# Gate products of two tiles as seven half-size block products, with the block sums on VectorE

## Chip, cores and metric

One core of one Trainium2 chip. The metric is the device time of one execution in microseconds (us); lower is better. All data are 32-bit floats.

## What is computed

A two-layer latent block with a small context stream, followed by a third attention block. The change touches one place of the two layers, the gated merge of three branches:

```
def merge_branches(o_a, o_b, o_c, gate_logits, w_branch, w_out):
    g_a, g_b, g_c = jnp.split(jax.nn.sigmoid(gate_logits), 3, axis=-1)
    merged = g_a * (o_a @ w_branch[0]) + g_b * (o_b @ w_branch[1]) + g_c * (o_c @ w_branch[2])
    return merged @ w_out
...
p = h @ w_in[l]                 # the last 3 * 1024 columns of p are the gate logits
...
mod = silu_c @ w_ada[l] + b_ada[l]      # 6 * 1024 modulation values for each layer
```

`h` has 1024 features. The first layer (`l = 0`) works on 512 latent and 256 context tokens together, 768; the second (`l = 1`) on 512 at this place.

## The kernel before

Every engine gets its own instruction list, unrolled from one list of jobs, `PLAN[l]`, that `plan_layer` writes for each layer (the job's first word is its kind). Each engine runs its part of the jobs strictly in that order, and semaphores tie the engines together: `full`/`free` for the PSUM places, and an `event` counter for each kind of result. On VectorE and ScalarE, `V.do`/`A.do` also wait for each instruction's own end before the next.

The dense part of a layer comes after attention: four `conv_b` jobs, and then for the branches 2, 0 and 1 and the eight 128-feature tiles of each a `gate` job and a `branch` job. On TensorE (PE) a `gate` is 8 matmuls deep (1024 input features) over all tokens; a matmul handles at most 512 tokens, so in layer 0 it is 8 of 512 and 8 of 256 columns. A `branch` is 4 deep. ScalarE (ACT) takes the sigmoid of a gate tile into one of two places of `probT`, and VectorE (DVE) multiplies it with the branch product and adds it into `merged`. Then `gate_used` says that the place of `probT` is free.

In layer 0, `with_modulation` spreads 40 `acc` jobs over the dense part. Each is four VectorE instructions on a 128x1024 piece of `w_ada` that multiply it by the conditioning vector and add it up (`accumulate`). After four of them, a `rsum` (PE sums over partitions, ACT copies) and an `adag` (PE turns, DVE writes `mod`) finish the group.

Weights arrive through `ring`, six places of 1 MB. SyncE (SP) issues the loads in the order of first use; the load into a place waits until the piece that was there has been used (`chunk_prev`, `chunk_end`). `gate` pieces hold two tiles, and so do `branch` pieces.

Of the kernel before, what the change touches and what calls it, by code (L numbers as in the profile page):

```python
# [105 lines left out]
def program(nc, x, c, ctx_in, c_ctx, w_ada, b_ada, g_mix, g_ffn, w_in, qg_a, kg_a, qg_b, kg_b, sink_b, conv_w,  # L106
            w_branch, w_out, w_router, w_e_gate, w_e_up, w_e_down, norm_gain_2, w_in_2, q_norm_a_2, k_norm_a_2,
            sinks_a_2, q_norm_b_2, k_norm_b_2, w_out_2, consts, out):
    with ExitStack() as stack:
# [96 lines left out]
        back = [obuf[:, n * D:(n + 1) * D] for n in (3, 4, 5)] + [merged[:, n * D:(n + 1) * D] for n in (1, 2, 3)]  # L206
        iota = con[:, C_IOTA:C_IOTA + NX]
# [225 lines left out]
        def plan_layer(l):  # L433
# [5 lines left out]
            gates = {br: [(w, l, br, d) for d in range(KD) for w in ("gate", "branch")] for br in range(3)}  # L439
            dense = conv + gates[2] + gates[0] + gates[1]  # L440
# [12 lines left out]

        PLAN = {0: plan_layer(0), 1: plan_layer(1), 2: plan_second()}
# [10 lines left out]
        def event(name, keys):  # L465
            return Count(sem(name), keys)
# [39 lines left out]
        sig_ready = event("gate_sigmoid", of("gate", "silg"))  # L506
# [169 lines left out]
        chunk_key = {}  # L676

# [89 lines left out]
        def chunk_of(j):  # L767
# [13 lines left out]
            if kind == "gate":  # L781
                return ("gate", l, t, j[3] // 2), j[3] % 2
# [39 lines left out]
        WEIGHTED = ("qk", "v", "conv_c", "conv_x", "conv_b", "gate", "branch", "silg", "side", "wout", "wt")  # L822
# [113 lines left out]
        def _(pe):  # L936
# [81 lines left out]

            def run(j):
# [40 lines left out]
                elif kind in ("conv_c", "conv_x") or kind == "silg" and j in job:  # L1060
                    pass
                elif kind in ("qk", "conv_b", "gate", "silg", "branch", "wout"):
# [693 lines left out]
        def _(act):  # L1756
# [59 lines left out]
            def run(j):  # L1816
# [849 lines left out]
```

## Time and profile before

| | |
|---|---|
| time, median of 3 runs | 3112.27 us (3110.53 to 3115.92) |
| the profiled execution | 3114.2 us, its span 3112.4 us |
| PE busy | 2984.3 us, 96% |
| DVE busy | 1052.1 us, 34% |
| ACT busy | 613.1 us, 20% |
| layer 0, dense part | 438.14 to 872.34 us of the span |
| layer 1, gates and branches | 1950.3 to 2194.2 us, less the first gates |

Busy shares are means over stages with different limits. What a change is worth in one stage is read from that stage's instructions in order of time: which engine had something to wait for, and for whom.
### The profile page before, as it was taken

What the parts mean: (1) busy time and instruction counts of PE and PEld (TensorE: products, weight loads), DVE (VectorE), ACT (ScalarE), POOL (GpSimd) and SP (SyncE); (2) the same over time, 40 slices, a digit from 0 to 9 for tenths busy, and PEclk for the clock granted to TensorE, in tenths of its full rate; (3) what the DMA queues carried; (4) which work ended last, traced back from release to release, by engine and by line L of the source; (5) the groups of instructions that cost most, each with busy time, mean ns of one, the idle gap of its engine ahead of it and who ended that gap; (6) DMA issues with size and microseconds to landing.
All of it is one profiled execution on the core that took longest, in us unless ns stands there. A gap on an engine that the chain in (4) does not pass through costs nothing.

```text
span 3112.4 us, 32607 instructions
## 1 busy us (share of the span) xinstructions
PE 2984.3 (96%) x13043; PEld 1404.1 (45%) x13043; DVE 1052.1 (34%) x1566; ACT 613.1 (20%) x1121; POOL 75.0 (2%) x88
## 2 busy tenths in 40 slices
PE   7999999999999999999999999999979898899999
PEld 4565655555545222222335655444433222234547
DVE  4764645556514000000147554011121010137352
ACT  3135530000003010111031453000011101021161
POOL 1000000000000010101000000000000000000000
PEclk9999999999999999999999999999999999999999
DMA  8120013434413999999870201222489999963200
GB/s 251 41 82 14 15 55 128 176 135 157 161 41 140 397 351 380 355 371 380 298 200 1 68 21 46 68 81 95 162 333 408 408 408 407 408 221 81 68 1 28
DMA packets 266076, 578.83 MB, mean 186 GB/s; under 512 B 62040, under 2 KB 140136, under 8 KB 265800
## 3 DMA queue, kind: packets, MB, share of 16 engines
q1 hardware_dynamic: 258064, 554.09, 48.8%
q0 software_dynamic: 7552, 22.61, 2.4%
q8 instruction: 106, 1.74, 0.2%
q14 instruction: 42, 0.34, 0.0%
q10 hardware_dynamic: 312, 0.05, 0.0%
HBM read 561.49 MB, written 15.20 MB: 185 GB/s over the span
## 4 chain that ended last, share of the span: by engine, by line
PE 84%; DMA 11%; DVE 3%; issue 1%; ACT 1%; SPq 0%; DVEq 0%; POOL 0%; ACTq 0%; POOLq 0%
PE ps L1016 31%; PE ps L1420 9%; PE ps L1535 6%; PE ps L1032 5%; PE ps L1432 5%; PE ps L1080 5%; PE ps L1248 3%; PE ps L1260 3%; PE ps L1294 3%; DMA ring<-in_w_e_up 3%; PE ps L1093 2%; DMA ring<-in_w_e_down 2%; DMA ring<-in_w_e_gate 2%; PE ps L1056 2%; PE ps L1476 2%; PE ps L1230 1%
## 5 line engine op out<-in xcount | busy, mean ns | idle before, releaser
L1016 PE MATMUL ps<-hT,ring 128*128 128x512 f32 (+1 forms) x2080 | 773.2, 529 | 3.0 <-ACT hT L1761 2.9
L1016 PEld LDWEIGHTS ps<-hT,ring 128*128 128x128 f32 x2080 | 394.9, 191 | 367.6 <-issue 343.7
L1420 PE MATMUL ps<-ring,hT 128*64 128x512 f32 x1392 | 333.1, 607 | 17.2 <-DMA ring<-in_w_e_up 11.9
L1420 PEld LDWEIGHTS ps<-ring,hT 128*64 128x64 f32 x1392 | 89.7, 137 | 220.1 <-issue 219.3
L1032 PE MATMUL ps<-hT,ring 128*128 128x512 f32 (+1 forms) x448 | 181.5, 533 | 0.7 <-DVEq L1746 0.7
L1761 ACT ACTIVATE prob<-ps 128x512 f32<-128x512 f32 (+1 forms) x67 | 46.4, 693 | 681.0 <-PE ps L1016 681.0
L1432 PE MATMUL ps<-ring,hT 128*32 128x512 f32 x1392 | 167.4, 598 | 0.5 <-ACT hT L1761 0.5
L1535 PE MATMUL ps<-ring,hT 128*64 128x512 f32 x640 | 150.4, 603 | 15.0 <-DMA ring<-in_w_e_down 10.8
L1761 ACT ACTIVATE prob<-prob,nms 128x768 f32<-128x768 f32 (+5 forms) x224 | 159.2, 711 | 18.9 <-DVE nms L2384 8.6
L1080 PE MATMUL ps<-merged,ring 128*128 128x512 f32 (+1 forms) x384 | 142.7, 526 | 3.1 <-issue 3.1
L1016 PE MATMUL ps<-obuf,ring 128*128 128x512 f32 (+1 forms) x384 | 143.4, 523 | 0.0
L1260 PE MATMUL ps<-con,prob 128*128 128x128 f32 x872 | 140.2, 283 | 1.3 <-DVE merged L2408 0.5
L1260 PEld LDWEIGHTS ps<-con,prob 128*128 128x128 f32 x872 | 96.4, 140 | 89.5 <-issue 78.8
L2534 DVE TENSOR_TENSOR qbuf<-qbuf,ps 128x1536 f32<-128x1536 f32 x8 | 14.0, 1754 | 341.1 <-ACT qbuf L1761 341.1
L1761 ACT ACTIVATE hT<-ps,mod,amp 128x256 f32<-128x256 f32 (+1 forms) x96 | 50.7, 528 | 327.7 <-PE ps L1470 182.1
L2596 DVE SCALAR_TENSOR_TENSOR xT<-ps,mod,xT 128x512 f32<-128x512 f32 x40 | 30.0, 751 | 249.2 <-PE ps L1476 248.8
L1925 ACT COPY merged<-ps 128x512 f32<-128x512 f32 (+1 forms) x128 | 71.5, 559 | 169.9 <-PE ps L1260 129.9
L2296 DVE TENSOR_TENSOR prob<-prob,ps 128x768 f32<-128x768 f32 (+1 forms) x32 | 26.2, 820 | 231.6 <-PE ps L1016 231.6
L1248 PE MATMUL ps<-kbuf,obuf 64*128 64x256 f32 (+2 forms) x576 | 100.9, 464 | 2.5 <-DVEq L1746 2.2
L1080 PEld LDWEIGHTS ps<-merged,ring 128*128 128x128 f32 x384 | 71.2, 190 | 70.5 <-issue 67.4
L1016 PEld LDWEIGHTS ps<-obuf,ring 128*128 128x128 f32 x384 | 72.4, 190 | 66.2 <-issue 63.3
L1294 PE MATMUL ps<-merged,vbuf 128*64 128x256 f32 x736 | 96.7, 390 | 0.9 <-DVE merged L2408 0.9
(333 smaller groups left out, 3029.0 us busy)
## 6 DMA issues: line engine op xcount, KB each, us to landing
ring<-in_w_e_gate SPq DMA_DIRECT2D x95, 1024.0 KB, 12.3
ring<-in_w_e_up SPq DMA_DIRECT2D x83, 1024.0 KB, 9.7
ring<-in_w_e_down SPq DMA_DIRECT2D x76, 1024.0 KB, 9.4
ring<-in_w_in SPq DMA_DIRECT2D x49, 1024.0 KB, 5.3
ring<-in_w_ada SPq DMA_DIRECT2D x48, 1024.0 KB, 7.3
ring<-in_w_e_down SPq DMA_DIRECT2D x32, 512.0 KB, 7.2
ring<-in_w_in SPq DMA_DIRECT2D x48, 256.0 KB, 4.7
merged<-in_w_e_up SPq DMA_DIRECT2D x12, 1024.0 KB, 15.1
```

What stands on the lines that cost most here:

```text
L1016: mm = pe.matmul(ps[:, b + a:b + e], lhs[:, k, :], rhs[:, k, a:e], start=k == 0, stop=k == nk - 1)
L1032: mm = pe.matmul(ps[:, BANK[SIDE]:BANK[SIDE] + hi - lo], ring3(slot)[:, k, m % 2 * P:(m % 2 + 1) * P], h3[:, k, lo:hi], start=k == 0, stop ...
L1056: mm = pe.matmul(ps[:, b:b + CH], o2[:, k, t * P:(t + 1) * P], ring3(slot)[:, k, :], start=k == 0, stop=k == KD - 1)
L1080: mm = pe.matmul(ps[:, b:b + e - a], w[:, k, :], m3[:, k, a:e], start=k == 0, stop=k == KD - 1)
L1248: mm = pe.matmul(ps[:, b[a] + c0:b[a] + c0 + w], q[r, u["g"], u["q0"]:u["q0"] + P], k[r, u["kj"], k0:k0 + w], start=True, stop=True)
L1260: mm = pe.transpose(ps[:, o:o + P], scored(j[1], j[2], a, u)[:, m * P:(m + 1) * P], ident)
L1294: mm = pe.matmul(out_, v(tiles[m], col), exp_, start=m == 0, stop=m == len(tiles) - 1, tile_position=(0, a * HD))
L1420: mm = pe.matmul(ps[e * CX:(e + 1) * CX, b + h * 512:b + (h + 1) * 512], lhs, second_weights(slot_of[sub], e, h), start=k == 0, stop=k == ...
L1432: mm = pe.matmul(ps[q:q + CC, b + 1024:b + 1536], lhs, second_weights(slot_of[k % 2], e, h), start=k == 0, stop=k == KD - 1, tile_position ...
L1535: mm = pe.matmul(to, lhs[:, k, s0:s0 + CX], second_weights(slot, e, h), start=k == 0, stop=k == KD - 1, tile_position=(0, e * CX))
L1761: return sc.activation(o, i, f, **kw)
L1925: A.do(sc.copy(*turned_to(j)), tb_done[r], j)
```

## The change

Two gate tiles of one ring piece become one job `gate2`. The 1024 input features are cut into two halves, the two tiles are two halves of the output features, and the tokens are cut into two halves. A product of 2x2 by 2x2 blocks needs eight block products; the change computes seven, of sums of blocks:

```
P1 = A11 B11    P2 = A12 B21    P3 = S4 B22    P4 = A22 T4
P5 = S1 T1      P6 = S2 T2      P7 = (A11 - A21)(B22 - B12)
```

Here A are the weight blocks, B the token blocks, S sums of weight blocks and T sums of token blocks. A block product is 4 matmuls of 384 columns in layer 0 and of 256 in layer 1. PE runs them in the order 1, 6, 5, 7, 2, 4, 3 and accumulates some of them on top of others in PSUM, after VectorE has read what was there. The parts:

- `hsum`, once a layer on VectorE: the sums of token blocks (3 instructions on all of 4 feature groups, 4 on one each). PE waits for it before the first P1.
- `wsum`, once a pair on VectorE: 4 instructions of 512 columns, the sums of weight blocks. It stands between the two `branch` jobs of the pair before. PE waits for it before P6.
- `gate2` on VectorE: 5 instructions of half the tokens (`u2`, `u3`, `22`, `21`, `12`), on ACT one copy and four sigmoids. P7 waits for `u2`, P2 for the copy, P4 for `u3`, P3 for `22`; `u2` waits for P6, `u3` for P7, `21` for P4, `12` for P3.
- In layer 0 the last two ring places hold sums of token blocks, so the dense part's loads go round four places.
- `with_modulation` counts a `gate2` as two jobs and puts no `acc` behind a `wsum` or behind the second `branch` of a pair.

```diff
@@ with_modulation
+            def long(j):
+                return {"hsum": 0, "wsum": 0, "gate2": 2}.get(j[0], 1)
...
-            count, passed, share = len(todo), 0, len(jobs) - 4
+            count, passed, share = len(todo), 0, sum(map(long, jobs)) - 4
...
-                passed += 1
+                passed += long(j)
                 while due and due[0][0] <= passed:
                     order.append(due.pop(0)[1])
+                if j[0] == "wsum" or j[0] == "branch" and j[3] % 2:
+                    continue
                 while todo and (count - len(todo)) * share < passed * count:
@@ plan_layer
-            gates = {br: [(w, l, br, d) for d in range(KD) for w in ("gate", "branch")] for br in range(3)}
-            dense = conv + gates[2] + gates[0] + gates[1]
+            pairs = [(l, br, n) for br in (2, 0, 1) for n in range(KD // 2)]
+            dense = conv + [("hsum", l), ("wsum",) + pairs[0]]
+            for at, (_, br, n) in enumerate(pairs):
+                dense += [("gate2", l, br, n), ("branch", l, br, 2 * n)]
+                dense += [("wsum",) + p for p in pairs[at + 1:at + 2]] + [("branch", l, br, 2 * n + 1)]
@@ loads, layer 0: places of the ring from hsum to the first wout
+                        if few[0]:
+                            add_chunk(key, chunk_dmas(key), few[1] % (RING - 2))
+                            few[1] += 1
@@ TensorE
+                times("p1", a, w[:, 0:4, 0:P], h3[:, 0:4, 0:half], True)
+                need(weight_sums_ready, ("wsum",) + j[1:])
+                times("p6", b, s2, t2, True)
+                times("p5", c, s1, t1, True)
+                need(seven_added, j[1:] + ("u2",))
+                times("p7", b, w[:, 0:4, P:2 * P], h3[:, 0:4, half:2 * half], False)
+                need(first_product, j[1:])
+                times("p2", a, w[:, 4:8, 0:P], h3[:, 4:8, 0:half], False)
+                need(seven_added, j[1:] + ("u3",))
+                times("p4", b, w[:, 4:8, P:2 * P], t4, False)
+                need(seven_added, j[1:] + ("22",))
+                times("p3", c, s4, h3[:, 4:8, half:2 * half], False)
@@ VectorE
+                elif kind == "hsum":
+                    V.do(v.tensor_tensor(t1, b12, b11, ALU.subtract))
+                    V.do(v.tensor_tensor(t2, b22, t1, ALU.subtract))
+                    for k in range(4):
+                        V.do(v.tensor_tensor(t4[k], b21[:, k, :], t2[:, k, :], ALU.subtract))
+                    V.do(v.tensor_tensor(b12, b22, b12, ALU.subtract), token_sums_ready, j)
+                elif kind == "wsum":
+                    dve.wait_ge(w_full[slot], value)
+                    V.do(v.tensor_tensor(s1, a21, a22, ALU.add))
+                    V.do(v.tensor_tensor(s2, s1, a11, ALU.subtract))
+                    V.do(v.tensor_tensor(s4, a12, s2, ALU.subtract))
+                    V.do(v.tensor_tensor(a21, a11, a21, ALU.subtract), weight_sums_ready, j)
+                elif kind == "gate2":
+                    V.need(first_product, j[1:])
+                    V.need(seven_full, j[1:] + ("p6",))
+                    V.do(v.tensor_tensor(c12, p1, second, ALU.add), seven_added, j[1:] + ("u2",))
+                    V.need(seven_full, j[1:] + ("p7",))
+                    V.do(v.tensor_tensor(c22, p1, second, ALU.add), seven_added, j[1:] + ("u3",))
+                    V.do(v.tensor_tensor(c22, c22, third, ALU.add), seven_added, j[1:] + ("22",))
+                    V.need(seven_full, j[1:] + ("p4",))
+                    V.do(v.tensor_tensor(p1, p1, second, ALU.add), seven_added, j[1:] + ("21",))
...
+                    V.need(seven_full, j[1:] + ("p3",))
+                    V.do(v.tensor_tensor(c12, c12, third, ALU.add), seven_added, j[1:] + ("12",))
```

The order of VectorE in layer 0, in the middle of branch 2. Before, between two tiles (`merged<-prob,ps` is the end of a `branch`; four instructions on `ring,silc` are one `acc`; `mod` is `adag`):

```order
L2293 TENSOR_TENSOR merged<-prob,ps 128x768
L2171 TENSOR_TENSOR mod<-ps,pv 128x8 x2
L2159 SCALAR_TENSOR_TENSOR vbuf<-ring,silc,vbuf 128x1024 x4
L2293 TENSOR_TENSOR merged<-prob,ps 128x768
L2159 SCALAR_TENSOR_TENSOR vbuf<-ring,silc,vbuf 128x1024 x4
L2157 TENSOR_SCALAR kbuf<-ring,silc 128x1024
L2157 TENSOR_SCALAR prob<-ring,silc 128x1024
L2159 SCALAR_TENSOR_TENSOR kbuf<-ring,silc,kbuf 128x1024
L2159 SCALAR_TENSOR_TENSOR prob<-ring,silc,prob 128x1024
L2293 TENSOR_TENSOR merged<-prob,ps 128x768
```

After the change, from the third pair's `12` (the first row, which waits for P3) to the `wsum` of the fourth pair (the last four rows):

```order
L2414 TENSOR_TENSOR prob<-prob,ps 128x384
L2259 TENSOR_TENSOR mod<-ps,pv 128x8 x2
L2247 SCALAR_TENSOR_TENSOR vbuf<-ring,silc,vbuf 128x1024 x8
L2422 TENSOR_TENSOR merged<-prob,ps 128x768
L2245 TENSOR_SCALAR kbuf<-ring,silc 128x1024
L2245 TENSOR_SCALAR prob<-ring,silc 128x1024
L2247 SCALAR_TENSOR_TENSOR kbuf<-ring,silc,kbuf 128x1024
L2247 SCALAR_TENSOR_TENSOR prob<-ring,silc,prob 128x1024
L2394 TENSOR_TENSOR kbuf<-ring 128x512
L2395 TENSOR_TENSOR vbuf<-kbuf,ring 128x512
L2396 TENSOR_TENSOR prob<-ring,vbuf 128x512
L2397 TENSOR_TENSOR ring<-ring 128x4x128
```

All `acc` instructions of a pair now stand between the last sum of one pair and the weight sums of the next; over the whole of layer 0 there are 36 `acc` jobs in eleven such stretches (2, 4, 3, 3, 4, 3, 3, 4, 3, 3 and 4), and the other four stand ahead of `hsum`.

The order of TensorE at a similar place. Before, two tiles, each a gate of 8 and 8 matmuls and a branch of 4 and 4 (`qbuf` holds the convolution's output; the L1150 row is an `adag`):

```order
L1016 MATMUL ps<-hT,ring 128x512 x8
L1016 MATMUL ps<-hT,ring 128x256 x8
L1150 MATMUL ps<-con,sq_rs 128x4 x4
L1016 MATMUL ps<-qbuf,ring 128x512 x4
L1016 MATMUL ps<-qbuf,ring 128x256 x4
L1016 MATMUL ps<-hT,ring 128x512 x8
L1016 MATMUL ps<-hT,ring 128x256 x8
L1016 MATMUL ps<-qbuf,ring 128x512 x4
L1016 MATMUL ps<-qbuf,ring 128x256 x4
```

After, one pair: P1; P6; P5; P7 and P2 (the row of 8); P4 in two rows; P3; the `adag`; and two branches:

```order
L1080 MATMUL ps<-hT,ring 128x384 x4
L1080 MATMUL ps<-ring,vbuf 128x384 x4
L1080 MATMUL ps<-ring,kbuf 128x384 x4
L1080 MATMUL ps<-hT,ring 128x384 x8
L1080 MATMUL ps<-ring 128x384 x2
L1080 MATMUL ps<-sq_rs,ring 128x384 x2
L1080 MATMUL ps<-hT,prob 128x384 x4
L1231 MATMUL ps<-con,sq_rs 128x4 x4
L1058 MATMUL ps<-qbuf,ring 128x512 x4
L1058 MATMUL ps<-qbuf,ring 128x256 x4
L1058 MATMUL ps<-qbuf,ring 128x512 x4
L1058 MATMUL ps<-qbuf,ring 128x256 x4
```

The gates of both tiles now stand ahead of both branches, so between P3 of one pair and P6 of the next, PE has two branches and P1 to run.

The order of SP's loads behind the first pair, before (each row one piece of weights; `w_in` are gates, `w_ada` accumulations; in brackets, whose progress the load waits for):

```order
L1598 DMA ring<-in_w_ada 128x2x1024 [waits psum_full0]
L1598 DMA ring<-in_w_ada 128x2x1024 [waits modulation_chunk_used]
L1598 DMA ring<-in_w_in 128x8x256 [waits modulation_chunk_used]
L1598 DMA ring<-in_w_ada 128x2x1024 [waits psum_full1]
L1598 DMA ring<-in_w_branch 128x4x256 [waits modulation_chunk_used]
```

And after:

```order
L1682 DMA ring<-in_w_in 128x8x256 [waits seven_products_full]
L1682 DMA ring<-in_w_ada 128x2x1024 [waits modulation_chunk_used]
L1682 DMA ring<-in_w_ada 128x2x1024 [waits psum_full2]
L1682 DMA ring<-in_w_ada 128x2x1024 [waits modulation_chunk_used]
L1682 DMA ring<-in_w_branch 128x4x256 [waits seven_products_full]
```

With four places, the fourth load behind a gate piece waits for that pair's P3, which here is the next pair's gate piece and then that pair's own branch piece.

## Rows read from the trace of the kernel before

**Rows 1.** The page: busy times of the engines, and PE in 40 slices (tenths)

```profile
PE 2984.3 (96%) x13043; PEld 1404.1 (45%) x13043; DVE 1052.1 (34%) x1566; ACT 613.1 (20%) x1121; POOL 75.0 (2%) x88
...
PE   7999999999999999999999999999979898899999
```

**Rows 2.** Busy times in the two dense parts (window, length, engines, clock, DMA, GB/s)

```profile
438.14:872.34 434.20, 434.18 (x1523) 255.37 (x1521) 240.16 (x229) 26.59 (x35) 0.00 (x0) 1.00 0.42 144
1950.30:2194.20 243.90, 243.90 (x569) 107.75 (x567) 26.17 (x38) 15.61 (x25) 0.00 (x0) 1.00 0.25 76
```

**Rows 3.** Timeline of PE, layer 0 (start, length, instruction; idle before it in brackets)

```profile
675.92 10.59 PE L1016 MATMUL ps<-hT,ring 128*128 128x512 f32 x32
686.35 5.32 PE L1016 MATMUL ps<-obuf,ring 128*128 128x512 f32 x16
691.60 0.64 PE L1140 MATMUL ps<-kbuf,ones 128*32 128x256 f32 x8
...
703.02 0.95 PE L1150 MATMUL ps<-con,sq_rs 128*128 128x4 f32 x8
```

**Rows 4.** Timeline of PE: layer 1, and sixteen matmuls of 256 columns in layer 0

```profile
2008.72 7.03 PE L1016 MATMUL ps<-hT,ring 128*128 128x512 f32 x16
2015.58 3.60 PE L1016 MATMUL ps<-qbuf,ring 128*128 128x512 f32 x8
...
952.76 7.07 PE L1080 MATMUL ps<-merged,ring 128*128 128x256 f32 x32
959.77 0.61 PE L1177 MATMUL ps<-xT,prob 128*16 128x256 f32 x2
```

**Rows 5.** Timeline of DVE in layer 0

```profile
661.76 0.37 DVE L2171 TENSOR_TENSOR mod<-ps,pv 128x8 f32<-128x8 f32 x2
...
670.20 1.28 DVE L2159 SCALAR_TENSOR_TENSOR kbuf<-ring,silc,kbuf 128x1024 f32<-128x1024 f32 x1
671.52 1.29 DVE L2159 SCALAR_TENSOR_TENSOR prob<-ring,silc,prob 128x1024 f32<-128x1024 f32 x1
676.04 0.95 DVE L2296 TENSOR_TENSOR prob<-prob,ps 128x768 f32<-128x768 f32 x1 [3.23 <-PE ps L1016]
...
678.13 1.28 DVE L2159 SCALAR_TENSOR_TENSOR kbuf<-ring,silc,kbuf 128x1024 f32<-128x1024 f32 x1
...
683.41 1.54 DVE L2157 TENSOR_SCALAR vbuf<-ring,silc 128x1024 f32<-128x1024 f32 x2
```

**Rows 6.** DVE groups by form, 438 to 2200 us (busy, mean ns, idle before)

```profile
L2534 DVE TENSOR_TENSOR qbuf<-qbuf,ps 128x1536 f32<-128x1536 f32 x8 | 14.0, 1754 | 341.1 <-ACT qbuf L1761 341.1
...
L2330 DVE TENSOR_TENSOR hT<-hT 128x512 f32<-128x512 f32 x7 | 4.8, 692 | 0.9
...
L2204 DVE TENSOR_TENSOR hT<-xT,sq_rs 128x256 f32<-128x256 f32 x8 | 3.4, 426 | 0.3
```

**Rows 7.** Timeline of PE around its longest idle time

```profile
2280.39 1.04 PE L956 MATMUL ps<-of_expert,prob 128*128 128x16 f32 x4 [12.13 <-DVE prob L2457]
2282.34 5.41 PE L950 MATMUL ps<-con 128*128 128x512 f32 x8 [0.91 <-DVEq L1750]
...
40.76 19.50 PE L1016 MATMUL ps<-hT,ring 128*128 128x512 f32 x46 [2.22 <-ACT hT L1761]
```

**Rows 8.** Windows at the same places; the granted clock stands behind POOL

```profile
42.00:46.00 4.00, 4.00 (x5) 1.43 (x5) 3.83 (x5) 3.83 (x6) 0.00 (x0) 0.50 1.01 269
46.00:50.00 4.00, 4.00 (x10) 1.86 (x9) 3.66 (x9) 3.80 (x7) 0.00 (x0) 0.92 0.98 221
...
2270.00:2275.00 5.00, 0.00 (x0) 0.00 (x0) 4.76 (x10) 0.00 (x0) 0.00 (x0) 0.72 1.01 387
...
2280.00:2285.00 5.00, 3.70 (x7) 2.10 (x8) 0.81 (x5) 0.00 (x0) 1.67 (x2) 0.50 0.65 213
2285.00:2290.00 5.00, 3.00 (x8) 1.16 (x7) 0.00 (x0) 0.00 (x0) 0.31 (x1) 0.92 0.56 196
```

**Rows 9.** DMA issues in layer 0's gates (KB each, median us to landing)

```profile
ring<-in_w_ada SPq DMA_DIRECT2D x23, 1024.0 KB, 7.3
```

More of the change, by code:

```diff
@@ L676, in program @@
         chunk_key = {}
+        few, after_sums = [False, 0], []
         def second_place(r):
@@ L780, in chunk_of @@
                 return (kind, l, t // 2), t % 2
-            if kind == "gate":
-                return ("gate", l, t, j[3] // 2), j[3] % 2
+            if kind in ("gate2", "wsum"):
+                return ("gate", l, t, j[3]), 0
             if kind == "branch":
@@ L820, in chunk_dmas @@
             return plain(w_out[l], n * CH)
-        WEIGHTED = ("qk", "v", "conv_c", "conv_x", "conv_b", "gate", "branch", "silg", "side", "wout", "wt")
+        WEIGHTED = ("qk", "v", "conv_c", "conv_x", "conv_b", "gate2", "wsum", "branch", "silg", "side", "wout", "wt")
         def chunk_keys(j):
@@ L1017, in product, with seven_products, times @@
                 part(mm, key)
+            def seven_products(j):
+                l = j[1]
+                half = (NT, NX)[l] // 2
+                cn, slot = weights(chunk_of(j)[0])
+                if j[1:] == PAIRS_FIRST[l]:
+                    need(oT_ready, ("O", l, 2 * TILES[l] - 1))
+                    need(token_sums_ready, ("hsum", l))
+                a = begin(j)
+                b = a + 512
+                third = (HEAD_SUMS, SIDE)[j[3] % 2]
+                c = begin(j + ("c",), third)
+                w = ring3(slot)
+                s1, s2, s4 = weight_sums
+                t1, t2, t4 = token_sums[l]
+                def times(name, bank, lhs, rhs, first):
+                    for k in range(4):
+                        mm = pe.matmul(ps[:, bank:bank + half], lhs[:, k, :], rhs[k] if name == "p4" else rhs[:, k, :],
+                                       start=first and k == 0, stop=k == 3, skip_group_check=not first)
+                    mm.then_inc(seven_full.sem, 1)
+                times("p1", a, w[:, 0:4, 0:P], h3[:, 0:4, 0:half], True)
[10 more added lines that the diff above has]
+                times("p3", c, s4, h3[:, 4:8, half:2 * half], False)
+                chunk_end[cn] = (seven_full.sem, seven_full.at[j[1:] + ("p3",)])
             def run(j):
@@ L1059, in run @@
                     chunk_end[cn] = (full[job[j][0]], job[j][2])
-                elif kind in ("conv_c", "conv_x") or kind == "silg" and j in job:
+                elif kind in ("conv_c", "conv_x", "hsum", "wsum") or kind == "silg" and j in job:
                     pass
-                elif kind in ("qk", "conv_b", "gate", "silg", "branch", "wout"):
+                elif kind == "gate2":
+                    seven_products(j)
+                elif kind in ("qk", "conv_b", "silg", "branch", "wout"):
                     ck, m = chunk_of(j)
@@ L1573, in load @@
                     sp.wait_ge(done, value)
+                for since, place in after_sums:
+                    if n >= since and slot == place and (chunk_prev[n] is None or chunk_prev[n] < since):
+                        sp.wait_ge(seven_full.sem, seven_full.at[LAST_PAIR[0] + ("p3",)])
                 if n - LOOPC[0] in FIRST_PLACES:
```

83 lines of the change are left out of this document (67 added, 16 removed).

## Prediction

> **What bounds the kernel now.** I read the page first: PE is busy 96% of the span and 9 tenths or more in nearly every slice, DVE 34% [rows 1]. So PE sets the time nearly everywhere, and the first question is what its columns cost. Then the windows of the two dense parts: PE fills both (434.18 of 434.20 us in layer 0), at full clock, with DMA at 0.42 and 0.25 [rows 2]. The same row says something that the page's mean hides: in layer 0's dense part DVE is busy 240 of 434 us, because the accumulations (`acc`) run there; in layer 1 it is 26 of 244. Last, the timeline of DVE: after its accumulations it waits for PE (3.23 us at 676.04) [rows 5]. Its slack is only useful if its work stands where PE doesn't wait for it. That is what the change alters.
>
> **PE's work.** A layer 0 gate takes 686.35 - 675.92 = 10.43 us for 8 x 768 = 6144 columns, 1.70 ns a column; a branch 691.60 - 686.35 = 5.25 us [rows 3]. A layer 1 gate takes 6.86 us for 4096 columns, 1.675 ns; sixteen matmuls of 256 columns take 7.01 us, 1.71 ns [rows 4]. So small matmuls lose only 2% here. A block product of layer 0 (4 x 384 columns, no row of that width) I put at 1.69 ns, between these: 2.60 us; of layer 1 (4 x 256) 1.75 us. Seven of them are 18.2 us against 20.9 for two gates, and 12.25 against 13.7. Twelve pairs: 32 us less in layer 0 and 17.5 us less in layer 1, 49 us in all. Alone, this would be the gain.
>
> **VectorE's new work.** Durations of a two-operand instruction: 1.75 us for 1536 columns, 0.69 for 512, 0.43 for 256 [rows 6], and 0.95 for 768 [rows 5], on one straight line of about 0.16 us + 1.04 ns a column; 384 columns lie at 0.56 us, 1024 at 1.23 us. From one instruction to the next pass 0.04 us (671.52 - 670.20 = 1.32 for one of 1.28), and DVE starts 0.12 us behind the start of PE's next work (676.04 against 675.92) [rows 3, 5]; I take up to 0.3 us for such a step, since the end of a matmul is modelled. So `wsum` is 4 x 0.73 = 2.9 us; `12` is 0.6 us; an accumulation is 4 x 1.32 = 5.3 us, or 4.2 for the first of a group, whose first two instructions take 0.77 each [rows 5]; `hsum` is 3 x 1.79 + 4 x 0.60 = 7.8 us in layer 0, and 3 x 1.27 + 4 x 0.47 = 5.7 us in layer 1. ACT's copy and sigmoids (half a tile each) lie beside products of 2.6 us, and I cost them at nothing; if that cover were gone they would cost some 0.5 us each.
>
> **The start of each dense part.** PE must wait for `hsum` before the first P1, with nothing else to run. In layer 0, DVE first reads the last `conv_b` (0.3 + 1.1), then has one accumulation (5.3), then `hsum` (7.8): 14.5 us idle, and `wsum` outlasts P1 by 0.3. In layer 1: 0.3 + 0.8 + 5.7 = 6.8, and `wsum` (2.9) outlasts P1 (1.75) by 1.2: 8.0 us.
>
> **The loop in layer 0.** This term decides. From P6 to P3 of a pair, DVE is held by `gate2`: each of its sums waits for a product, so in these 6 x 2.60 = 15.6 us it works under 3 us and can't take an accumulation, since its list is in order. Everything else stands between P3 of one pair and P6 of the next, and P6 waits for `wsum`, the end of that list (the order of DVE after the change). Over the eleven stretches: hops, `12` and `wsum` 0.3 + 0.6 + 2.9 + 0.1 = 3.9 each, 43 us; the first `branch` of a pair, 1.1 us in branch 2 (four) and 2.1 us in the others (seven), 19 us; 36 accumulations, 9 x 4.2 + 27 x 5.3 = 181 us; nine `adag`, each 0.5 us of DVE [rows 5], and for the eight that stand directly behind P3 about 1.2 us until PE has made them (0.95 us [rows 3] and a step), 15 us. Sum 258 us, 23.5 a stretch. PE has two branches and P1 to run meanwhile, 2 x 5.25 + 2.6 = 13.1 us, and in most stretches an `rsum` or an `adag` of about 1 us. So PE idles 8 to 10 us in every pair, part of it before P1 or a branch, most before P6. P2, P4 and P3 don't wait: each has a product of 2.6 us between it and a sum of 0.6.
>
> Layer 0's dense part after: `conv_b` 41.7 + start 14.5 + P1 and rest of `wsum` 3.0 + 12 x 15.6 = 187 + 258 + the last two branches and `adag` 11.5 = 516 us, against 434.2 [rows 2]: **+82 us**. Layer 1: there are no accumulations. From P3, DVE needs 0.3 + 0.5 + 1.5 + 2.9, and must wait for the first branch (3.4 us); `wsum` is ready 8.1 us behind P3, when PE has just done two branches and P1 (8.6 us). No stall, but a cover of only half a microsecond. So -17.5 + 8.0 = **-9.5 us**.
>
> **The clock.** After PE's idle time from 2268.3 the granted clock had fallen within 2270 to 2275 (mean 0.72, so about 4 us in), and was 0.50, the 1.2 GHz level, when matmuls came again; it was back some 3.5 us into the dense work that begins at 2282.34 (0.92 over 2285 to 2290 leaves 0.8 us at half). At 40.76, after 2.2 us idle and sparse work before, it stayed at 0.50 for 5.8 us [rows 7, 8]. At half clock half the time is lost: 1.7 to 2.9 us a fall, 2.3 in the middle. The stalls come to 13 places (eleven stretches, two starts), and P6 follows them on the path. All falling costs 30 us; I take three of four, since the idle times before P6 are 4 to 7 us and the trace shows the fall at 4: **+22 us**. The Trainium skill's page "TensorE: Matmul & The Clock Gate", section "HAM oscillation — how this bites in real kernels", says that a wait between bursts drops the engine to half rate every time, and that the price is paid at each burst. By that rule alone the sum would be 8 us higher; the one long idle time of this trace agrees with it.
>
> **The ring of four.** The load that waits for P3 is issued then and lands 7.3 us later [rows 9]. Where it is a branch piece, PE's first branch starts about 7 us late, and ends 12.6 us behind P3; DVE comes to it at about 13, behind its accumulations. Where it is an accumulation's, DVE wants it 10 us behind P3 or later. I take nothing, hidden under the DVE's own list; without that cover it costs up to 7.3 us a stretch.
>
> **Sum.** +82 - 9.5 + 22 = +94 us on the profiled execution's 3114.2 us (1.8 us around its span), 3208; that execution lies 1.9 us above the median of 3112.27, so the forecast is 3206 us.
>
> **The rivals.**
> (a) The same loop, but the clock holds, because short products before and after the idle times keep it up. +82 - 9.5 = +72: 3185 us. For it: idle time is cut into pieces of 1 to 7 us. Against: the fall about 4 us into an idle time, and at 40 us after only 2.2.
> (b) PE stays the bound, and the change is a gain. The 49 us less 14.5 + 0.3 + 8.0 of the starts is -26: 3086 us. That needs DVE's list between P3 and P6 to fit into about 15 us; the turning point, no change, is 17 to 18 us a stretch (26 us over eleven). The list is 23.5 by rows, and the two terms that make it, the number of accumulations and 5.3 us for one, are certain. Only if DVE were free before P3 could it be; its order forbids it.
> (c) Late pieces. If the ring of four also holds up DVE, 11 x 7.3 = up to 80 us more: up to 3285 us, half of that 3245. Against: the first two or three pieces behind a gate's piece don't wait for P3.
> (d) The products are slower than 1.69 ns a column, because 84 of them in each layer begin with a wait and change operands. If each loses 0.2 us, 72 + 84 on the path, +31 us: 3237 us. Against: gates and branches change operands too, at no visible gap (686.35 follows 675.92 without idle time) [rows 3].
> That the change doesn't do what it says is excluded by the order: the columns are gone from PE's list.
>
> **Chances.** Forecast (loop, most clocks fall; 3192 to 3225) 0.62; (a) 0.19; (c) 0.07; (d) 0.07; (b) 0.05. The range from 3170 to 3235 holds the first two and the lower parts of (c) and (d). A difference under about 0.2% (6 us) can't be told from none. Faster 0.04, within it 0.01, slower 0.95.
>
> **What would show it.** In the profile after: layer 0's dense part 500 to 550 us long instead of 434; PE idle before P6 in each pair with DVE's `wsum` as releaser, 4 to 7 us; DVE without idle time between `12` and `wsum`, except before an `adag`; windows of P6 with a granted clock below 1; one idle time of about 14 us and one of about 7 before the first P1 of each layer; layer 1's pairs at about 19.1 us without idle time. The prediction is wrong if DVE waits for DMA in the stretches, if the accumulations take under 4 us, or if PE's idle time before P6 is under 2 us.

## The result, and the profile after

| | before | after |
|---|---|---|
| time, median | 3111.4 us (3109.62 to 3115.92, 4 runs) | 3205.76 us (3205.02 to 3206.93, 4 runs) |
| the profiled execution's span | 3112.4 us | 3203.2 us |
| mean granted clock | 0.994 | 0.977 |

The ratio is 1.0303 (95% interval 1.0288 to 1.0318): the change makes the kernel 94 us slower. The forecast was 3206 us.

First the page after; its lines answer to [rows 1]. Busy times and the slices, then the chain that ended last, then the groups of P6 (`ps<-ring,vbuf` of 384 columns is P6 and nothing else):

```profile
PE 2970.5 (93%) x13235; PEld 1454.0 (45%) x13235; DVE 1189.8 (37%) x1796; ACT 634.3 (20%) x1193; POOL 75.1 (2%) x88
...
PE   7999997877879999999999999999979988999999
...
PE 77%; DMA 11%; DVE 10%; issue 2%; ACT 1%; SPq 0%; DVEq 0%; POOL 0%; ACTq 0%; POOLq 0%
...
L1080 PE MATMUL ps<-ring,vbuf 128*128 128x384 f32 x96 | 55.3, 745 | 64.4 <-DVE ring L2397 64.4
```

PE has only 14 us less to do than before (2970.5 for 2984.3), although 49 us of columns are gone: part of it came back as matmuls at half clock. A mean over the span hides the damage: DVE is busy only 37% of it. The damage shows in one stage, the slices 7 to 12 (layer 0's dense part), where PE has 7 and 8 instead of 9, and in the chain, of which DVE holds 10%, against 3% in the page before:

```profile
PE 84%; DMA 11%; DVE 3%; issue 1%; ACT 1%; SPq 0%; DVEq 0%; POOL 0%; ACTq 0%; POOLq 0%
```

A P6 record takes 745 ns. P5, the product behind it, also of 384 columns, takes 496 (groups by form, layer 0's dense part of after); the first product behind the wait is the slow one:

```profile
L1080 PE MATMUL ps<-ring,kbuf 128*128 128x384 f32 x96 | 33.8, 496 | 0.0
```

Below, a product at half clock is called cold, and one at full clock warm.

Second, windows of after (length, then busy time and count of PE, weight loads, DVE, ACT and POOL, then the granted clock, DMA share, GB/s): layer 0's dense part, which answers to [rows 2]; a P6 at half clock; the only P6 behind a wait that was warm; and layer 1's dense part with its `conv_b`:

```profile
437.95:977.25 539.30, 440.71 (x1426) 251.00 (x1424) 314.10 (x344) 37.60 (x71) 0.00 (x0) 0.90 0.33 112
648.05:653.33 5.28, 5.28 (x8) 2.87 (x9) 0.93 (x1) 0.48 (x1) 0.00 (x0) 0.50 0.26 108
...
530.05:532.74 2.69, 2.69 (x9) 1.63 (x10) 0.93 (x1) 0.48 (x1) 0.00 (x0) 1.00 1.01 416
2021.50:2285.69 264.19, 257.52 (x930) 177.68 (x929) 93.51 (x158) 25.37 (x61) 1.07 (x2) 0.99 0.26 79
```

Layer 0's dense part is 539.3 us instead of 434.2 (+105.1). Layer 1's is 264.2 instead of 274.9 (-10.7; before, its first `conv_b` starts at 1919.35 and its last branch ends at 2194.21).

Third, the waits of PE in layer 0's dense part of after, and those of DVE in the eleven stretches between its pairs (us in total, times, longest):

```profile
PE ps L1080 <- DVE ring L2397: 64.4, 11, 7.8
PE ps L1080 <- issue: 14.4, 1, 14.4
PE ps L1058 <- DMA ring<-in_w_branch: 10.9, 4, 3.9
PE ps L1080 <- DMA ring<-in_w_in: 3.8, 4, 1.6
```

```profile
DVE prob L2407 <- PE ps L1080: 51.2, 11, 5.0
DVE prob L2410 <- PE ps L1080: 44.2, 11, 4.0
DVE prob L2405 <- PE ps L1080: 36.7, 11, 4.7
DVE prob L2414 <- PE ps L1080: 21.5, 11, 2.0
```

The two views belong together. PE waits before each of eleven P6 for L2397, the last instruction of `wsum`. DVE waits 154 us inside the pairs, for the products of `gate2` (four of its lines, eleven times each). Each engine stands idle while the other works, and no wait of DVE for a DMA is in its list. Between the pairs DVE waits for an `adag` (8.3 us in eight) and once, in the first stretch, 1.6 us for the first branch.

Last, DVE and PE from one pair's P3 to the next one's P6, in order of time:

```profile
626.46 0.55 DVE L2414 TENSOR_TENSOR prob<-prob,ps 128x384 f32<-128x384 f32 x1 [1.96 <-PE ps L1080]
627.24 0.37 DVE L2259 TENSOR_TENSOR mod<-ps,pv 128x8 f32<-128x8 f32 x2 [0.23 <-PE ps L1231]
...
628.18 1.28 DVE L2247 SCALAR_TENSOR_TENSOR kbuf<-ring,silc,kbuf 128x1024 f32<-128x1024 f32 x1
...
645.13 0.69 DVE L2394 TENSOR_TENSOR kbuf<-ring 128x512 f32<-128x512 f32 x1
...
647.30 0.69 DVE L2397 TENSOR_TENSOR ring<-ring 128x512 f32<-128x512 f32 x1
```

```profile
623.68 2.74 PE L1080 MATMUL ps<-hT,prob 128*128 128x384 f32 x8
...
627.07 10.57 PE L1058 MATMUL ps<-qbuf,ring 128*128 128x512 f32 x32
638.68 2.85 PE L1080 MATMUL ps<-hT,ring 128*128 128x384 f32 x8 [1.05 <-DMA ring<-in_w_in]
648.05 5.49 PE L1080 MATMUL ps<-ring,vbuf 128*128 128x384 f32 x8 [6.52 <-DVE ring L2397]
653.33 3.08 PE L1080 MATMUL ps<-ring,kbuf 128*128 128x384 f32 x8
```

P3 starts at 623.68 and ends at about 626.25. From there until 647.99 DVE has no gap longer than the 0.23 us before the `adag`, and P6 starts at 648.05: 21.8 us, in which PE had 10.57 + 2.7 us of work. P6 then takes 653.33 - 648.05 = 5.28 us, twice the 2.58 of a warm product, at a clock of 0.50.

Where the time went, stage by stage, in this and in all kernels of the experiments below. Each stage is read from PE's timeline, in the one profiled execution of a kernel: layer 0's dense part from the first matmul of `conv_b` to the row `ps<-mod,wr` behind the last branch, layer 1's likewise.

| kernel | layer 0 dense | between | layer 1 dense | behind | span |
|---|---|---|---|---|---|
| before | 434.2 | 1047.0 | 274.9 | 918.2 | 3112.4 |
| after | 539.3 | 1044.3 | 264.2 | 917.5 | 3203.2 |
| l1_only | 434.4 | 1048.8 | 264.5 | 918.1 | 3103.2 |
| acc_half | 442.9 | 1046.5 | 264.5 | 917.9 | 3108.5 |
| filler | 538.5 | 1044.2 | 264.3 | 917.5 | 3201.3 |
| filler_full | 518.9 | 1043.7 | 264.2 | 917.3 | 3181.0 |
| ring4_before | 491.2 | 1043.1 | 274.9 | 917.9 | 3164.3 |
| inside | 438.5 | 1042.7 | 263.9 | 917.2 | 3099.8 |
| l1_early | 434.5 | 1044.3 | 259.3 | 917.8 | 3092.8 |
| inside_early | 424.0 | 1044.8 | 257.6 | 917.4 | 3080.8 |
| inside_mid | 424.0 | 1046.2 | 257.7 | 917.6 | 3084.9 |
| inside_late0 | 421.0 | 1044.3 | 257.7 | 917.7 | 3077.6 |

The stage between the two dense parts is 1042.7 to 1048.8 us long, in kernels that have the same work there. So 3 us of a span say nothing here, and the dense parts are what can be compared.

### The profile page after: what moved, and what is told of

The parts are those of the page before. It is cut to its first block, busy times and chain, and to the rows that moved or that the text cites. A ratio compares the mean times of both kernels' runs of the same rounds, so it can differ in the third digit from the quotient of the medians.

```text
span 3203.2 us, 33437 instructions
## 1 busy us (share of the span) xinstructions
PE 2970.5 (93%) x13235; PEld 1454.0 (45%) x13235; DVE 1189.8 (37%) x1796; ACT 634.3 (20%) x1193; POOL 75.1 (2%) x88
## 3 DMA queue, kind: packets, MB, share of 16 engines
q8 instruction: 107, 1.75, 0.2%
## 4 chain that ended last, share of the span: by engine, by line
PE 77%; DMA 11%; DVE 10%; issue 2%; ACT 1%; SPq 0%; DVEq 0%; POOL 0%; ACTq 0%; POOLq 0%
PE ps L1058 14%; PE ps L1080 11%; PE ps L1501 8%; PE ps L1616 6%; PE ps L1111 5%; PE ps L1161 4%; PE ps L1513 4%; PE ps L1329 3%; PE ps L1341 3%; PE ps L1375 3%; DMA ring<-in_w_e_up 3%; PE ps L1174 2%; DVE vbuf L2247 2%; DMA ring<-in_w_e_gate 2%; DMA ring<-in_w_e_down 2%
## 5 line engine op out<-in xcount | busy, mean ns | idle before, releaser
L1058 PE MATMUL ps<-hT,ring 128*128 128x512 f32 (+1 forms) x928 | 352.1, 537 | 2.1 <-ACT hT L1845 2.1
L1058 PEld LDWEIGHTS ps<-hT,ring 128*128 128x128 f32 x928 | 176.8, 191 | 171.7 <-issue 156.3
L1080 PE MATMUL ps<-hT,ring 128*128 128x384 f32 (+1 forms) x576 | 167.2, 441 | 25.0 <-issue 21.1
L1111 PE MATMUL ps<-hT,ring 128*128 128x512 f32 (+1 forms) x448 | 181.5, 533 | 0.7 <-DVEq L1830 0.7
L1080 PEld LDWEIGHTS ps<-hT,ring 128*128 128x128 f32 x576 | 110.3, 193 | 78.3 <-issue 30.3
L1080 PE MATMUL ps<-ring,vbuf 128*128 128x384 f32 x96 | 55.3, 745 | 64.4 <-DVE ring L2397 64.4
## 6 DMA issues: line engine op xcount, KB each, us to landing
ring<-in_w_e_gate SPq DMA_DIRECT2D x95, 1024.0 KB, 10.5
```

Of the source, the lines that this page charges most:

```text
L1058: mm = pe.matmul(ps[:, b + a:b + e], lhs[:, k, :], rhs[:, k, a:e], start=k == 0, stop=k == nk - 1)
L1080: mm = pe.matmul(ps[:, bank:bank + half], lhs[:, k, :], rhs[k] if name == "p4" else rhs[:, k, :], start=first and k == 0, stop=k == 3, ski ...
L1111: mm = pe.matmul(ps[:, BANK[SIDE]:BANK[SIDE] + hi - lo], ring3(slot)[:, k, m % 2 * P:(m % 2 + 1) * P], h3[:, k, lo:hi], start=k == 0, stop ...
```

## The experiments

The theory is that of the forecast: VectorE's list between two pairs, mostly accumulations, is what P6 waits for, and the granted clock adds to it. The rivals are the clock that holds, late loads, slow products, and DVE's added work as such. "Before" was run beside each group of kernels: 3112.1 us in the first (16 runs), 3111.28 in the second (9), 3112.48 in the last (7).

### Seven products in layer 1 alone (l1_only)

```diff
             dense = conv + [("hsum", l), ("wsum",) + pairs[0]]
-            for at, (_, br, n) in enumerate(pairs):
+            if l == 0:
+                dense = conv + [(w, l, br, d) for br in (2, 0, 1) for d in range(KD) for w in ("gate", "branch")]
+            for at, (_, br, n) in enumerate(pairs if l else []):
```

> Seven products in layer 1 alone; layer 0's dense part, its accumulations and its ring as before. Theory (VectorE's list of layer 0 is the loss): layer 1's gates and branches from 274.9 to 264 us, the time about 3101 us, 0.35% less than before. Rival (a seven-product pair costs more than its columns save in any layer, by waits and small matmuls): no less than before, 3111 us or more.

Measured: 3102.48 us, ratio 0.9968 (0.9956 to 0.998); layer 1's dense part 264.5 us, 10.4 less than before, and layer 0's as before (434.4). The rows show a pair from P1 to the next P1, without a wait:

```profile
2052.38 1.89 PE L1081 MATMUL ps<-hT,ring 128*128 128x256 f32 x8
...
2064.47 7.03 PE L1059 MATMUL ps<-obuf,ring 128*128 128x512 f32 x16
2071.33 1.89 PE L1081 MATMUL ps<-hT,ring 128*128 128x256 f32 x8
```

A pair takes 2071.33 - 2052.38 = 18.95 us. Where DVE has no accumulations the change does what its products promise. All the loss of the whole change is in layer 0.

### Half of each accumulation (acc_half)

```diff
-                for k in range(2):
+                for k in (0,):
                     weight = ring3(slot, 2)[:, k, :]
```

> The changed kernel, with each of the 40 accumulations doing only its first two instructions instead of four: the second half of each piece of w_ada is left out of the modulation, though it is still loaded. Nothing else moves: same order, same four ring places, same loads and waits. Theory (the time of VectorE's list between P3 and P6): a stretch shrinks by 3.3 x 2.64 = 8.6 us from 23.5 to about 15, just what PE has to run, so layer 0's dense part falls from 539 to about 440 us and the time from 3206 to about 3105 us. Rival 1 (late pieces, the ring of four): the loads are the same, so layer 0 stays above 500 us and the time above 3170. Rival 2 (slow products): 36 idle times go, but 7 x 12 product starts stay at their price; not under 3130.

Measured: 3109.85 us, ratio 0.9992 (0.9983 to 1.0001). The waits of PE in layer 0's dense part, and one P6:

```profile
PE ps L1080 <- issue: 11.8, 1, 11.8
PE ps L1058 <- DMA ring<-in_w_branch: 11.1, 4, 3.9
...
PE ps L1080 <- DVE ring L2397: 0.7, 2, 0.5
```

```profile
620.45 2.85 PE L1080 MATMUL ps<-ring,vbuf 128*128 128x384 f32 x8 [0.19 <-DVE ring L2397]
```

Of 64.4 us of waits before P6 0.7 are left, and a P6 takes 2.7 us. So DVE's list is the cause: with half of the accumulations gone, nine of the eleven P6 don't wait at all. Of the miss of 5 us, 3 lie in layer 0, 442.9 us for about 440, and it is still longer than before: the start costs 11.8 us, and the waits for branch loads 11.1 us in four places. These were there in after as well (10.9), but beside DVE's list they cost nothing; here they are on the path, and the two branches behind each take 12.1 to 13.4 us instead of 10.5, cold at their start.

### Matmuls that only keep PE busy (filler, filler_full)

In front of P6's wait 2 or 3 matmuls of 512 columns whose results nothing reads:

```diff
+                at = [i[1:] for i in of("gate2") if i[1] == 0].index(j[1:]) if l == 0 else 0
+                keep_clock(b, 0 if at < 2 else 2 if at < 4 else 3)
                 need(weight_sums_ready, ("wsum",) + j[1:])
```

> The changed kernel, with two or three dummy matmuls of 512 columns (1.7 us each) in layer 0 before PE waits for the weight sums of a pair, in ten of the eleven pairs that wait, so that PE idles 1 to 4 us there instead of 4 to 8. No other work moves. Theory (idle time drops the clock, and P6 and P5 then run at half clock): the granted clock of layer 0's dense part rises from 0.90 to 0.97 or more, P6 takes 2.6 us instead of 4.2 to 5.3, layer 0 gets about 20 us shorter, the time about 3185 us. Rival (P6 is slow for its operands, weight sums just written by VectorE in three buffers): P6 stays at 4 to 5 us and the time at 3206, or a little more where the dummies run past the wait.

Measured: 3204.99 us, ratio 1.0299 (1.0283 to 1.0315), as after. A miss. Each of the matmuls took 0.86 us and not the 1.7 that I had put it at, so 1.3 to 5.2 us of idle time were left before a P6 where I had expected 1 to 4. In all it fell from 64.4 to 40.4 us, the clock of the dense part rose from 0.90 to 0.92 only, and nine of the eleven P6 still took 4.1 to 5.3 us. Rows of its timeline (a cold P6, and a warm one), and two windows, an idle time and the P6 behind it:

```profile
694.05 5.49 PE L1080 MATMUL ps<-ring,vbuf 128*128 128x384 f32 x8 [4.94 <-DVE ring L2399]
...
857.86 2.85 PE L1080 MATMUL ps<-ring,vbuf 128*128 128x384 f32 x8 [2.73 <-DVE ring L2399]
```

```profile
689.12:694.05 4.93, 0.00 (x0) 0.00 (x0) 4.72 (x7) 0.00 (x0) 0.00 (x0) 0.92 0.59 201
694.05:699.34 5.29, 5.29 (x9) 2.86 (x10) 1.90 (x2) 0.48 (x1) 0.00 (x0) 0.50 0.16 33
```

In 4.93 us of idle time the clock fell only at the end (mean 0.92), and the whole P6 behind it still ran at 0.50. So a shorter idle time is no cheaper, once the clock falls at all. But this left open whether P6 was slow for the clock or for its fresh operands. Hence the same with so many matmuls that nearly no idle time is left:

```diff
-                keep_clock(b, 0 if at < 2 else 2 if at < 4 else 3)
+                keep_clock(b, (0, 1, 4, 4, 7, 8, 8, 6, 6, 5, 8, 8)[at] if l == 0 else 0)
```

> The changed kernel, with 1 to 8 extra matmuls of 512 columns ahead of each wait of P6 in layer 0, so many that PE's idle time before P6 is under about 1 us (65 extra matmuls in all, nothing reads what they write). In the first filler experiment, which left 2.7 to 5.2 us of idle time in a pair, the granted clock still fell. Theory (the list of VectorE sets P6's start, and the clock adds to it what idle time costs): P6 starts when it did, takes 2.6 us in every pair instead of 4.2 to 5.3, dense part of layer 0 about 516 to 520 us instead of 539, time 3183 to 3187 us. Rival 1 (the first product behind a long wait is slow for its new operands, not for the clock): P6 stays at 4 to 5 us, time 3205 us. Rival 2 (PE itself, and not VectorE, sets the pace): the extra matmuls add their own 55 us, 3260 us.

Measured: 3185.23 us, ratio 1.0237 (1.0223 to 1.0251); layer 0 518.9 us. The same pair:

```profile
688.80 2.85 PE L1080 MATMUL ps<-ring,vbuf 128*128 128x384 f32 x8 [0.68 <-DVE ring L2399]
```

All eleven P6 take 2.69 us. So it was the clock, not the operands, and its price on the path is 539.3 - 518.9 = 20.4 us. The stretches from P3's end to P6's start are the same as in after to 0.01 us in every one (mean 23.36 us), with 56 us of matmuls put into them: PE's own work doesn't set them.

### The ring of four in the old order (ring4_before)

The kernel before, with its loads in layer 0's gates and branches going round four places instead of six:

```diff
+                if j == ("gate", 0, 2, 0):
+                    few[0] = True
+                elif few[0] and j[0] == "wout":
+                    few[0] = False
...
+                            add_chunk(key, chunk_dmas(key), few[1] % (RING - 2))
```

> The kernel before, with its loads from the first gate of layer 0 to the first output product going round four ring places instead of six, nothing else changed. Theory (the four places cost nothing by themselves as long as PE has 10 us of other work): the time of before, within 0.1%, 3108 to 3115 us; at most an idle time of 1 to 2 us before a branch. Rival (the ring of four is a cost of its own): PE idles 3 to 4 us for a branch piece in each third pair, 15 us or more, 3126 us.

Measured: 3164.83 us, ratio 1.0168 (1.0154 to 1.0182). A miss by 53 us. PE's waits in the dense part, its timeline, and the loads that SP issues there:

```profile
PE ps L1025 <- DMA ring<-in_w_in: 39.3, 11, 7.7
```

```profile
624.20 12.29 PE L1025 MATMUL ps<-hT,ring 128*128 128x512 f32 x32 [3.07 <-DMA ring<-in_w_in]
```

```profile
616.00 0.37 SPq L1607 DMA_DIRECT2D ring<-in_w_ada  x1
616.41 0.47 SPq L1607 DMA_DIRECT2D ring<-in_w_in  x1
```

The gate piece's load stands behind that of an accumulation piece, whose place comes free when the gate before is done: it goes out at 616.41, and the gate starts on it at 624.20, 7.8 us later. Only the branch that starts at 615.8 lies between (5.25 us, as in [rows 3]), so the gate waits 3.07 us. The gate behind the wait takes 12.2 us instead of 10.4, with a cold start; of the eleven gates seven are so. In the new order two branches lie at that place (10.5 us), which covers most of such a load. So the ring of four is not free as such. The changed kernel's order hides most of it: in acc_half, with that order and a short list of DVE, PE waits 11.1 us for loads, here 39.3. What is left DVE's late P6 hides.

### Accumulations inside the pairs (inside)

`gate2` on DVE in three parts, one accumulation in each gap between them and one behind the first branch of a pair, in place of three or four in a row behind P3:

```diff
+                dense += [("gate2", l, br, n), ("g2b", l, br, n), ("g2c", l, br, n), ("branch", l, br, 2 * n)]
...
+                n = (2, 2, 1, 0)[j[2]] if j[0] == "conv_b" else int(j[0] in ("gate2", "g2b") or j[0] == "branch" and j[3] % 2 == 0)
```

> Seven products in both layers, but in layer 0 VectorE's part of a pair is cut in three, with one accumulation behind u2 (in front of u3) and one behind 22 (in front of 21), and one behind the first branch of a pair; conv_b takes 2, 2, 1 and 0 accumulations. So two accumulations a pair lie beside products of PE and only one in the list between P3 and P6. Theory (the position of the accumulations in the in-order list is what costs, not their number and not the products): layer 0's dense part 428 to 436 us (434.2 in the kernel before, 539 in the changed one), some P6 and P4 waits of 1 to 3 us left, time 3092 to 3106 us. Rival (VectorE's added work itself, some 80 us more of it in layer 0, or its port, is too much wherever it stands): layer 0's dense part stays above 480 us, time above 3145 us.

Measured: 3100.5 us, ratio 0.9962 (0.9949 to 0.9976); layer 0 438.5 us, for 539.3. DVE in the middle of a pair: `u2`, an accumulation while PE runs P5 and P7, `u3` and `22`, another beside P4 and P3, then `21`:

```profile
619.97 0.55 DVE L2402 TENSOR_TENSOR prob<-prob,ps 128x384 f32<-128x384 f32 x1 [2.23 <-PE ps L1075]
620.56 5.25 DVE L2242 SCALAR_TENSOR_TENSOR vbuf<-ring,silc,vbuf 128x1024 f32<-128x1024 f32 x4
625.84 0.55 DVE L2405 TENSOR_TENSOR prob<-prob,ps 128x384 f32<-128x384 f32 x1
626.43 0.55 DVE L2406 TENSOR_TENSOR prob<-prob,ps 128x384 f32<-128x384 f32 x1
627.02 5.25 DVE L2242 SCALAR_TENSOR_TENSOR vbuf<-ring,silc,vbuf 128x1024 f32<-128x1024 f32 x4
632.30 0.55 DVE L2409 TENSOR_TENSOR prob<-prob,ps 128x384 f32<-128x384 f32 x1
```

DVE does exactly what it did in after (1189.7 and 1189.8 us busy), the products are the same, and 105 us are back. So it is the place of the accumulations in the list, neither their number nor DVE's added work. The stretch is 16.1 us on average, and the kernel is faster than before by 0.4%, which fits the turning point of 17 to 18 us that the prediction gave. Layer 0 alone is still 4 us longer than before (I expected 428 to 436): 16.8 us of waits for `wsum` are left, 8.1 before the first P1, and three P6 and the first P1 are still cold (4.3 to 4.4 us for 2.69, 4.9 for 2.58).

### Early sums (l1_early, inside_early, inside_mid, inside_late0)

All sums of token blocks but the last are made before `conv_b` (which doesn't need them), and P6 waits for the first two weight sums only, P7 for the other two:

```diff
+            early = [("hsuma", l)] if l in (1,) else []
+            return first + attention_order(l) + early + with_modulation(l, dense) + (tail_first, tail_second)[l]()
...
+                need(weight_sums_ready, ("wsum",) + j[1:] + (0,))
                 times("p6", b, s2, t2, True)
                 times("p5", c, s1, t1, True)
                 need(seven_added, j[1:] + ("u2",))
+                need(weight_sums_ready, ("wsum",) + j[1:] + (1,))
```

In layer 1 alone, on top of l1_only:

> Seven products in layer 1 alone (3102.5 us, 0.9968 of before), and there all sums of token blocks but the last are made before conv_b, and P6 waits for the first two weight sums only. Theory: the idle 6.7 us before the first P1 become about 2 us, and its cold P1 (3.5 us) warm (1.75 us), pairs unchanged at 18.95 us: 3094 to 3098 us. Rival (the early sums delay conv_b by what they save): 3102 us.

Measured: 3094.7 us, ratio 0.9945 (0.9932 to 0.9959); layer 1's dense part 259.3 us, 5.2 less than in l1_only. The idle time before the first P1 is 2.3 us instead of 6.7, but the clock still falls:

```profile
1945.72 2.85 PE L1082 MATMUL ps<-hT,ring 128*128 128x256 f32 x8 [2.31 <-issue]
1948.37 2.73 PE L1082 MATMUL ps<-hT,vbuf 128*128 128x256 f32 x8
1950.94 1.89 PE L1082 MATMUL ps<-hT,kbuf 128*128 128x256 f32 x8
```

P1 and P6 take 2.65 and 2.57 us instead of 1.73: the idle time was expected right, the warm P1 not.

In both layers, on top of inside:

> As the kernel with accumulations inside the pairs; besides, all sums of token blocks but the last are made before conv_b in both layers, and P6 waits for the first two weight sums only (P7 for the other two). Theory: the waits before the first P1 fall from about 8 to 14 us to about 2 to 3 us in layer 0 and from 6.7 to about 2 us in layer 1, P6's waits fall by up to 1.4 us a pair: 3070 to 3085 us. Rival (sums made early only move the wait: ahead of conv_b, VectorE's list is what conv_b waits for): as the kernel without it, 3092 to 3106 us.

Measured: 3083.92 us, ratio 0.9913 (0.9899 to 0.9926); layer 0 424.0 us. It stands inside the forecast range, with a wait that wasn't expected, in `conv_b` itself: the ring of four now begins ahead of it.

```profile
466.13 23.18 PE L1054 MATMUL ps<-hT,ring 128*128 128x512 f32 x64 [8.22 <-DMA ring<-in_w_in]
```

Two ways round it. The first has the early sums and the ring of four of layer 0 only from the third `conv_b`:

```diff
+            if l == 0:
+                dense[3:3] = [("hsuma", l)]
...
-                if j in (("hsuma", 0), ("hsum", 0)):
+                if j in (("conv_b", 0, 2), ("hsum", 0)):
```

> As the kernel with accumulations inside the pairs and early sums, which has one new wait of 8.2 us for a load in conv_b of layer 0, because its ring of four begins there. Here the early sums of layer 0 stand behind the third conv_b, the ring of four begins at the third conv_b, and conv_b takes 2, 2, 0 and 0 accumulations. Theory (in the ring of four a gate's or conv_b's load stands in order behind an accumulation's load; with six places at that point it is early enough): the 8.2 us and the cold matmuls behind them (2.2 us) go, 3072 to 3077 us. Rival (the ring of four holds up the third conv_b's load just as well): 3081 to 3085 us.

Measured: 3084.52 us, ratio 0.9908 (0.9892 to 0.9925): the rival's range. PE waits 5.3 us for the same load, now sent out at 460.38, when the second `conv_b` has ended, and 2.4 us for a late accumulation. The second leaves layer 0's token sums where they were, behind `conv_b`:

> As the kernel with accumulations inside the pairs and early sums, but the sums of token blocks of layer 0 stay behind conv_b (there the ring of four begins), those of layer 1 are early. Theory: the wait of 8.2 us for the load in conv_b and its cold matmuls go (-10.4 us), the idle time before the first P1 is 8.1 us again instead of 2.2, with a cold P1 (+7.5 us): 3079 to 3083 us. Rival (the wait for the load has nothing to do with where the sums stand): 3088 to 3093 us.

Measured: **3080.04 us, ratio 0.9895 (0.9879 to 0.9912)**, the fastest kernel of this study. No load is waited for in layer 0's dense part (the two longest of its waits):

```profile
PE ps L1076 <- issue: 8.1, 1, 8.1
PE ps L1076 <- DVE vbuf L2394: 4.4, 5, 1.2
```

The eleven stretches are 14.9 us on average and every P6 is warm. The misses with the ring, ring4_before and inside_mid, have in common that PE waits for a load that goes out only when an earlier product has ended, with too little other work in between. Why the third `conv_b` of inside_mid is such a place was not shown further.

## Why the prediction was right

**The loop in layer 0.** The prediction said "This term decides", and it did. The stretch from P3's end to P6's start was put at 258 us over eleven, 23.5 each; it is 257, 23.4 each (16.5 to 29.2). PE's idle time before P6 is 1.3 to 7.8 us, 5.9 on average (4 to 7 expected). The parts hold in the rows: `12` 0.55, four weight sums of 0.69 at steps of 0.73, an accumulation 5.3, a half-token sum 0.55 to 0.56 (0.56 from the line through [rows 5, 6]), P6 0.06 us behind `wsum`. Two instructions of 0.17 us on `amp` behind some `adag` were not counted, and that DVE would have no idle time but before an `adag` fails once, by 1.6 us in the first stretch. acc_half shows that the list is the cause, inside that its order is.

**The start.** 14.4 us idle in layer 0 for 14.5, 6.7 in layer 1 for 6.8. That `wsum` would outlast P1, by 0.3 and 1.2 us, didn't come: P1 is cold, takes 4.2 and 3.5 us, and covers it. So that time is counted once, under the clock.

**The products.** 2.58 us for 2.60 in layer 0, 1.73 for 1.75 in layer 1. Rival (d), slower products, is out: P7 and P2, P4 and P3 follow each other at these steps with changed operands. In layer 1 a pair is 18.95 us for 19.1. Twelve of them gain 19.8 us on the 20.6 of two tiles before, instead of 17.5, and the start takes 8.9 of it, clock and all (6.7 idle, P1 and P6 2.2 longer): about the -10.7 that stands where -9.5 did.

**The clock.** 22 us, from three falls of four at 2.3 us. Of the eleven P6 ten were cold, at 1.5 to 2.6 us each, 21.0 us in all; both first P1 were too (1.6 and 1.8). More falls than taken, and each a little cheaper: 24 us. filler_full measured 20.4 of it by taking the idle time of the eleven away; rival (a)'s 3185 us is just that kernel's 3185.2. The Trainium skill's page "TensorE: Matmul & The Clock Gate", section "HAM oscillation — how this bites in real kernels", lets each wait between bursts cost a ramp: this trace agrees in ten of eleven, and the eleventh idle time, of 1.33 us, didn't lower the clock. The reason given, "the idle times are 4 to 7 us and the trace shows the fall at 4", was too narrow: inside and filler show falls behind 2.3 to 2.7 us, and ring4_before one behind 1.5.

**The ring of four.** The sum took nothing, and in this kernel that holds: 10.9 + 3.8 us of waits for loads lie inside stretches that DVE sets. But the working stood on a piece landing 7.3 us after its issue at a branch, "up to 7.3 us a stretch" without the cover, and that was mis-sized: 7.3 us was the time of an accumulation piece in the kernel before, and in after the branch pieces land 3.7 to 3.8 us behind their issue, with PE waiting 3.9 us at most. Without the cover it is 1.0 us a stretch plus cold branches (acc_half), and 3.6 us a gate plus seven cold gates, 57 us in all, where the old order is kept (ring4_before), for which I had expected nothing. That the ring adds nothing to this kernel is right; that four places cost nothing in any order "as long as PE has 10 us of other work", as I expected for ring4_before, was wrong.

**Sum.** By the stages: +105.1 in layer 0 (82 and the clock's 21.0 + 1.6 by the terms), -10.7 in layer 1, -3.6 elsewhere, which no step explains and which lies inside what that stage differs by anyway. Rival (b), a gain to 3086 us with DVE's list inside 15 us, was excluded for this order, and is what another order gives: inside_late0, with 14.9 us a stretch, reaches 3080. That the forecast is met within 1 us is luck: with the clock's 22 us shared out by places, the stages are off by about +3, -3 and -4 us, the profiled executions differ by 90.8 us for the 94, and it is the medians that lie 94.4 apart. The mechanism and the size of its main term, 257 us for 258, are not luck.

**What stays open.** Why the first `conv_b` pieces can't be had earlier, and whether the 8.1 us before layer 0's first P1 can go without a new wait, was not tried further. What decides whether the clock falls behind an idle time of 1.5 to 3.3 us isn't settled either.

## What to carry to other kernels

An engine at 37% of the span can still be the bound, if its list is in order and its slack lies between instructions that wait for the busy engine: add up what stands in its list between two hand-overs and compare that with what the other engine has to do meanwhile. Before a change that makes one engine wait for the other several times a round, move the long work that nobody waits for into those waits; here that turned +94 us into -11, and with sums made earlier and P6 waiting for two weight sums only, into -32. And a ring with fewer places is judged by the one load that stands in order behind a place which comes free late, not by the mean share of DMA.

## What the runs showed of the hardware that was not expected

- The granted clock can fall behind short idle times, and how long they are hardly changes the price. Behind 1.90 us and less all P6 were warm (filler_full, inside); of idle times from 2.29 to 2.73 us some left a warm P6 (2.68 in inside, 2.73 in filler) and some a cold one (2.29 in inside, 2.67 in filler); behind 3.58 us and more all were cold. That is no bound for other products: of ring4_before's gates one was cold behind 1.52 us (12.1 us for 10.4) and one warm behind 3.29, and in acc_half the branches behind 1.84 and 1.91 us were cold. A cold P6 takes 4.1 to 5.3 us instead of 2.69, and the longest of these stand behind 3.95 and 4.94 us as well as behind 6.52 and 7.45. The two gates:

```profile
548.81 12.28 PE L1025 MATMUL ps<-hT,ring 128*128 128x512 f32 x32 [1.52 <-DMA ring<-in_w_in]
...
855.47 10.59 PE L1025 MATMUL ps<-hT,ring 128*128 128x512 f32 x32 [3.29 <-DMA ring<-in_w_in]
```

- A clock that fell only at the end of an idle time (a mean of 0.92 over 4.93 us is 0.8 us at half) stayed down for the 5.3 us of matmuls behind it.
